# Windowed attention with sinks: the rounding and the subtraction of a finished head pair move to the front of their slots

## The chip, the cores and the metric

The kernel runs on one core of a Trainium2 chip. The metric is the device time of one launch in microseconds (us): the median of 3 runs was 3144.57 us, the runs lying between 3141.83 and 3146.22 us. One more execution was recorded by the profiler; all rows below come from it.

## What is computed

The reference is a stack of four transformer layers over 512 tokens of width 1024. The change lies in one of them only, the attention of the second layer (a window of 128 keys and one learned sink per head), which runs once:

```python
def swa_sinks(q, k, v, sinks):       # 16 query heads, 4 key/value heads, head size 64, 4 blocks of 128 queries
    s = einsum("bnqkgd,bnjkd->bnkgqj", qb, kk) * scale      # each block sees its own and the previous 128 keys
    s = where(mask, s, -inf)
    m = maximum(max(s, axis=-1), sink)
    p = exp(s - m)
    p = p / (sum(p, axis=-1) + exp(sink - m))
    out = einsum("bnkgqj,bnjkd->bnqkgd", p, vv)
mix = swa_sinks(q, k, v, od_sinks) @ od_w_out
```

## The kernel before

The program is written by hand, one instruction list per engine, with semaphores between them; nothing is reordered by a scheduler. The whole network is a list of steps (matrix products, norms, attentions), and in front of and behind each attention stands a barrier of TensorE, ScalarE and VectorE. Products that must be exact to float32 are made of two-part numbers: a "high" part, the value rounded by a ScalarE copy, and a "low" part, the value less its high part, subtracted on VectorE (here and there on GpSimd). The output of the attention needs both parts too (y_hi, y_lo), as it is the input of the next matrix product.

The function `window()`, which exists once for each engine, is the attention in question. It works in slots numbered s, one per head, and the 16 heads are staggered over them. In slot s

- TensorE transposes the probabilities of head s-2 in two halves (L1162, `turn`), each into the same PSUM bank 6, makes the scores of head s+2 in between (L1151 to L1154, `scores`), and multiplies the transposed probabilities of head s-3 with its values (L1173, `values`, 8 matmuls into bank 7). The two heads of a pair write the two halves of bank 7's partitions. Before the first head of a pair, `values` waits for the semaphore `output_low` of the pair before, since it overwrites bank 7.
- ScalarE copies each transposed half out of bank 6 (L1786, `take`), and between the two copies computes the exponentials of head s (L1775, L1777, `probs`). In every even slot it rounds the queries of a pair that comes later (L1762, `q_high`), in three slots the keys (L1767, `k_high`).
- VectorE takes the row maxima of head s+1 (L2365 to L2368, `maxima`), divides the probabilities of head s-1 by their sum (L2375 to L2382, `scale`), and in odd slots subtracts the low part of queries (L2352, `low_q`), in three slots that of keys (L2358, `low_k`).
- GpSimd copies key rows (L800) eight times in the stage; it has no part in the outputs.

A finished pair has three more steps, in every odd slot from s=5 to s=19: ScalarE rounds bank 7 into y_hi (L1791, `y_high`, waits for `values_added` of both heads), VectorE subtracts it from bank 7 into y_lo (L2386, `sub_low`, waits for `output_high`), and then `values` of the next pair may write bank 7. Both heads of pair p are multiplied with their values by the end of TensorE's slot 2p+4; the next pair's first `values` is the last thing of TensorE's slot 2p+5. Its two waits are these:

```python
pe.wait_ge(e["taken"], past(2 * h + 2))
if par == 0:
    pe.wait_ge(e["output_low"], past(pair))
```

Each engine runs its list strictly in the written order, so the place of a step in the slot decides what is held up by its wait. The scores lie in three slices of PSUM (`window_scores`, h % 3) and the probabilities in four of SBUF (h % 4), so that a head's scores, maxima, exponentials, division and transposition are spread over five slots.

Of the kernel before, what the change touches and what calls it, by code (L numbers as in the profile page):

```python
# [115 lines left out]
def program(nc, a, out):  # L116
# [9 lines left out]
    def past(n):  # L126

        return n + CR

    with ctx:  # L130
# [77 lines left out]
        def zt(k, n=1):  # L208
            return Z[:, k * S:(k + n) * S] if isinstance(k, int) else Z[:, bass.ds(k * S, n * S)]

        def zrows(rows, k):
            return Z[rows, k * S:(k + 1) * S] if isinstance(k, int) else Z[rows, bass.ds(k * S, S)]
# [6 lines left out]
        def parts(mode):  # L219

            if mode == "dil":
                last = [whi[1][:, 0:S], whi[1][:, S:2 * S], kz_last[:, 0:S], wlo[1][:, 0:S], wlo[1][:, S:2 * S], kz_last[:, S:2 * S]]
                return ([qkt(g) for g in range(3)], [qkt(3 + g) for g in range(3)],
                        [[qkt(6 + g) for g in range(3)], last[0:3]], [[qkt(9 + g) for g in range(3)], last[3:6]])
            return ([qkt(k) for k in range(2)], [qkt(2 + k) for k in range(2)],
                    [[qkt(4 + 4 * par + k) for k in range(2)] for par in range(2)],
                    [[qkt(6 + 4 * par + k) for k in range(2)] for par in range(2)])
# [433 lines left out]
        def window_scores(h, b, n=1):  # L661

            o = 2 * (h % 3) * S + 2 * P * b
            return PS[:, o + P:o + 2 * P] if b == 0 else PS[:, o:o + 2 * P * n]

        def window_probs(h, b, n=1):
            t = TMP[:, h % 4 * WIDE:(h % 4 + 1) * WIDE]
            return t[:, 0:P] if b == 0 else t[:, P + 2 * P * (b - 1):P + 2 * P * (b - 1 + n)]
# [10 lines left out]
        def window_small(h, what):  # L679

            return sums8[:, 4 + 12 * what + 4 * (h % 3):8 + 12 * what + 4 * (h % 3)]
# [732 lines left out]
        def _(act):  # L1414
# [341 lines left out]
            def window():  # L1756
                e = wn
                q_hi, _, k_hi, _ = parts("window")

                def q_high(pair):  # L1760
                    act.wait_ge(e["scores"], past(2 * pair - 2))
                    act.activation(q_hi[pair % 2], zt(pair), ACT.Copy).then_inc(e["q_high"], 1)  # L1762

                def k_high(j):
                    r = HALF[j % 2]
                    act.wait_ge(e["scores"], past(4 * j - 4))
                    act.activation(k_hi[j % 2][j % 2][r, :], zrows(r, 8 + j // 2), ACT.Copy).then_inc(e["k_high"], 1)  # L1767

                def probs(h):

                    act.wait_ge(e["neg_max"], past(h + 1))
                    act.wait_ge(e["turned"], past(2 * h - 6))
                    act.wait_ge(e["scaled"], past(h - 2))
                    small = window_small(h, 0)
                    act.activation(window_small(h, 2), small, ACT.Exp, bias=sinkb[:, h:h + 1]).then_inc(e["sink"], 1)  # L1775
                    for b in range(NB):
                        ins = act.activation(window_probs(h, b), window_scores(h, b), ACT.Exp, bias=small[:, b:b + 1],  # L1777
                                             accum_out=window_small(h, 1)[:, b:b + 1])
                    ins.then_inc(e["probs"], 1)

                def take(h, half):

                    n = len(TURNS[4 * half:4 * half + 4]) * P
                    act.wait_ge(e["turned"], past(2 * h + half + 1))
                    act.wait_ge(e["values_added"], past(h - 1))
                    act.activation(window_turned(h)[:, half * S:half * S + n], bank[6][:, 0:n], ACT.Copy).then_inc(e["taken"], 1)  # L1786

                def y_high(pair):

                    act.wait_ge(e["values_added"], past(2 * pair + 2))  # L1790
                    act.activation(ch(yhi, pair), bank[7], ACT.Copy).then_inc(e["output_high"], 1)  # L1791

                k_high(0)
                q_high(0)
                q_high(1)
                for s in range(HEADS + 4):
                    if 2 <= s < HEADS + 2:
                        take(s - 2, 0)
                    if s < HEADS:
                        probs(s)  # L1800
                    if 2 <= s < HEADS + 2:
                        take(s - 2, 1)
                    if s >= 4 and s % 2:
                        y_high((s - 4) // 2)
                    if s % 2 == 0 and s // 2 + 2 < HEADS // 2:
                        q_high(s // 2 + 2)
                    for j in range(1, 4):
                        if s == max(4 * j - 5, 0):
                            k_high(j)
# [169 lines left out]
        def _(dve):  # L1979
# [365 lines left out]
            def window():  # L2345
                e = wn
                q_hi, q_lo, k_hi, k_lo = parts("window")

                def low_q(pair):
                    dve.wait_ge(e["q_high"], past(pair + 1))  # L2350
                    dve.wait_ge(e["scores"], past(2 * pair - 2))
                    dve.tensor_tensor(q_lo[pair % 2], zt(pair), q_hi[pair % 2], ALU.subtract).then_inc(e["q_low"], 1)  # L2352

                def low_k(j):
                    r = HALF[j % 2]
                    dve.wait_ge(e["k_high"], past(j + 1))
                    dve.wait_ge(e["scores"], past(4 * j - 4))
                    dve.tensor_tensor(k_lo[j % 2][j % 2][r, :], zrows(r, 8 + j // 2), k_hi[j % 2][j % 2][r, :], ALU.subtract).then_inc(e["k_low"], 1)  # L2358

                def maxima(h):  # L2360

                    dve.wait_ge(e["scores"], past(h + 1))
                    dve.wait_ge(e["probs"], past(h - 2))
                    dve.wait_ge(e["neg_max"], past(h))
                    dve.tensor_reduce(window_max[:, 0:1], window_scores(h, 0), AX.X, ALU.max)  # L2365
                    dve.tensor_reduce(window_max[:, 1:NB], window_scores(h, 1, NB - 1).rearrange("p (b n) -> p b n", b=NB - 1), AX.X, ALU.max).then_inc(e["reduced"], 1)
                    dve.wait_ge(e["reduced"], past(h + 1))
                    dve.tensor_scalar(window_small(h, 0), window_max, sinkb[:, h:h + 1], -1.0, ALU.max, ALU.mult).then_inc(e["neg_max"], 1)  # L2368

                def scale(h):  # L2370

                    inv = window_small(h, 1)
                    dve.wait_ge(e["sink"], past(h + 1))
                    dve.wait_ge(e["probs"], past(h + 1))
                    dve.tensor_tensor(inv, inv, window_small(h, 2), ALU.add).then_inc(e["summed"], 1)  # L2375
                    dve.wait_ge(e["summed"], past(h + 1))
                    dve.reciprocal(inv, inv).then_inc(e["inverted"], 1)
                    dve.wait_ge(e["inverted"], past(h + 1))
                    dve.tensor_scalar(window_probs(h, 0), window_probs(h, 0), inv[:, 0:1], None, ALU.mult)
                    rows = window_probs(h, 1, NB - 1).rearrange("p (b n) -> p b n", b=NB - 1)  # L2380
                    by_block = inv[:, 1:NB].rearrange("p (b o) -> p b o", o=1).to_broadcast([P, NB - 1, 2 * P])
                    dve.tensor_tensor(rows, rows, by_block, ALU.mult).then_inc(e["scaled"], 1)  # L2382

                def sub_low(pair):
                    dve.wait_ge(e["output_high"], past(pair + 1))
                    dve.tensor_tensor(ch(ylo, pair), bank[7], ch(yhi, pair), ALU.subtract).then_inc(e["output_low"], 1)  # L2386

                low_k(0)
                low_q(0)
                low_q(1)  # L2390
                maxima(0)
                for s in range(HEADS + 4):
                    if s + 1 < HEADS:
                        maxima(s + 1)
                    if 1 <= s < HEADS + 1:
                        scale(s - 1)
                    if s >= 4 and s % 2:
                        sub_low((s - 4) // 2)
                    if s % 2 and s // 2 + 2 < HEADS // 2:
                        low_q(s // 2 + 2)  # L2400
                    for j in range(1, 4):
                        if s == max(4 * j - 5, 0):
                            low_k(j)
# [267 lines left out]
```

## Time and profile before

| what | value |
|---|---|
| median of 3 runs | 3144.57 us |
| the profiled execution's own time | 3139.92 us |
| its span | 3138.0 us |
| TensorE matmul busy in the span | 2925.7 us, 93% |
| VectorE, ScalarE, GpSimd busy | 1729.9, 1222.5, 1105.0 us |
| mean granted TensorE clock | 0.97 |

The span is the time from the first to the last instruction on the core; 1.9 us of the profiled execution's time lie outside of it. The attention in question runs from about 820 to 928 us. A matmul's recorded time is modelled, so a busy TensorE can hold small gaps; idle times are printed in square brackets, with the engine and line that ended them. In windows, PEclk is the granted TensorE clock as a share of 2.4 GHz: 1.00 is that, 0.50 is 1.2 GHz.

### The profile page before, as it was taken

The numbers are of one execution on the slowest core, as the hardware profiler recorded it, in microseconds if no ns is written. First come the engines' busy times: TensorE is split into PE (matmuls) and PEld (weight loads), VectorE is DVE, ScalarE is ACT, GpSimd is POOL, SyncE is SP. The second block draws the span as 40 slices with busy tenths as digits, with TensorE's granted clock in tenths as the row PEclk, the third lists the DMA queues.
The fourth block names the chain that finished last, engine by engine and source line by source line (L and its number), as shares of the span: only waits on it lengthen the run. The fifth ranks groups of instructions, "written<-read, shape, count | busy, mean of one in ns | idle before, by whom it ended". The sixth has DMA issues, their size and how long they took to land.

```text
span 3138.0 us, 39991 instructions
## 1 busy us (share of the span) xinstructions
PE 2925.7 (93%) x13704; PEld 2385.4 (76%) x13704; DVE 1729.9 (55%) x2176; ACT 1222.5 (39%) x2056; POOL 1105.0 (35%) x484
## 2 busy tenths in 40 slices
PE   5989999999879999999679999999899998999999
PEld 4767778877657888888458888888777897788887
DVE  7575757474546553764755333576275726563333
ACT  2564432233544322344443222466445654332221
POOL 3311444443214444443224444444202431044443
PEclk9998999998989999999889999999899999999999
DMA  5243445451002333332013333232102220033332
GB/s 195 83 150 124 154 128 194 141 160 63 28 21 81 94 100 94 89 94 88 1 34 94 95 98 96 88 95 89 48 1 62 88 88 8 15 100 94 94 94 94
DMA packets 364859, 278.85 MB, mean 89 GB/s; under 512 B 13363, under 2 KB 320948, under 8 KB 363700
## 3 DMA queue, kind: packets, MB, share of 16 engines
q1 hardware_dynamic: 363472, 276.76, 28.8%
q8 instruction: 79, 1.29, 0.2%
q14 instruction: 57, 0.46, 0.0%
q10 hardware_dynamic: 1251, 0.33, 0.0%
HBM read 274.96 MB, written 2.10 MB: 88 GB/s over the span
## 4 chain that ended last, share of the span: by engine, by line
PE 62%; issue 6%; DVE 3%; ACT 2%; POOL 1%; DVEq 0%; ACTq 0%; POOLq 0%
PE banks L993 12%; PE banks L988 12%; PE banks L997 12%; PE banks L945 6%; PE banks L951 6%; PE banks L948 6%; PE banks L1173 1%; PE banks L920 1%; PE banks L1355 1%; PE banks L1287 1%; PE banks L990 1%; ACT tmp L1777 0%; PE banks L1162 0%; PE banks L1335 0%; ACT tmp L1906 0%
## 5 line engine op out<-in xcount | busy, mean ns | idle before, releaser
L815 POOL TENSOR_TENSOR w_lo<-w_raw,w_hi 128x1024 fp32r<-128x1024 f32 (+1 forms) x424 | 1046.2, 2468 | 1831.2 <-ACT w_hi L1484 1830.2
L1484 ACT ACTIVATE w_hi<-w_raw 128x1024 fp32r<-128x1024 f32 (+1 forms) x424 | 445.6, 1051 | 1126.9 <-PE banks L997 824.0
L945 PE MATMUL banks<-w_hi,h_hi 128*128 128x512 f32 x960 | 387.5, 404 | 10.5 <-ACT h_hi L1661 7.2
L948 PE MATMUL banks<-w_hi,h_lo 128*128 128x512 f32 x960 | 378.7, 394 | 3.7 <-DVE h_lo L511 3.7
L951 PE MATMUL banks<-w_lo,h_hi 128*128 128x512 f32 x960 | 379.1, 395 | 0.8 <-POOL w_lo L815 0.7
L988 PE MATMUL banks<-h_hi,w_hi 128*128 128x512 f32 x1280 | 340.2, 394 | 10.0 <-ACT h_hi L1668 9.8
L993 PE MATMUL banks<-h_lo,w_hi 128*128 128x512 f32 x1280 | 319.3, 390 | 1.6 <-DVE h_lo L511 1.6
L988 PEld LDWEIGHTS banks<-h_hi,w_hi 128*128 128x128 f32 x1280 | 242.6, 190 | 65.6 <-issue 13.9
L997 PE MATMUL banks<-h_hi,w_lo 128*128 128x512 f32 x1152 | 284.5, 389 | 0.0
L993 PEld LDWEIGHTS banks<-h_lo,w_hi 128*128 128x128 f32 x1280 | 240.2, 188 | 55.2 <-DVE h_lo L511 5.7
L997 PEld LDWEIGHTS banks<-h_hi,w_lo 128*128 128x128 f32 x1152 | 216.2, 188 | 44.9
L945 PEld LDWEIGHTS banks<-w_hi,h_hi 128*128 128x128 f32 x960 | 198.0, 206 | 43.4 <-issue 12.4
L988 PE MATMUL banks<-mid_hi,w_hi 128*128 128x512 f32 x864 | 218.0, 391 | 12.8 <-ACT mid_hi L1608 6.8
L948 PEld LDWEIGHTS banks<-w_hi,h_lo 128*128 128x128 f32 x960 | 198.4, 207 | 35.9 <-DVE h_lo L511 4.2
L951 PEld LDWEIGHTS banks<-w_lo,h_hi 128*128 128x128 f32 x960 | 197.8, 206 | 36.5 <-POOL w_lo L815 2.0
L993 PE MATMUL banks<-mid_lo,w_hi 128*128 128x512 f32 x864 | 218.6, 392 | 1.3 <-DVE mid_lo L2128 1.1
L997 PE MATMUL banks<-mid_hi,w_lo 128*128 128x512 f32 x864 | 215.0, 390 | 0.0
L2145 DVE TENSOR_TENSOR xT<-banks,xT 128x512 f32 (+1 forms) x80 | 55.3, 692 | 280.6 <-PE banks L997 280.6
L988 PEld LDWEIGHTS banks<-mid_hi,w_hi 128*128 128x128 f32 x864 | 162.1, 188 | 52.3 <-ACT mid_hi L1608 9.4
L993 PEld LDWEIGHTS banks<-mid_lo,w_hi 128*128 128x128 f32 x864 | 162.7, 188 | 39.6 <-DVE mid_lo L2138 3.5
L997 PEld LDWEIGHTS banks<-mid_hi,w_lo 128*128 128x128 f32 x864 | 162.8, 188 | 33.8
L2233 DVE TENSOR_TENSOR tmp<-tmp,head_sums 128x512 f32<-128x512 f32 (+1 forms) x84 | 133.4, 1588 | 36.0 <-issue 24.5
(311 smaller groups left out, 4505.4 us busy)
## 6 DMA issues: line engine op xcount, KB each, us to landing
w_raw<-in_m_w_up SPq DMA_DIRECT2D x64, 512.0 KB, 3.9
w_raw<-in_m_w_down SPq DMA_DIRECT2D x64, 512.0 KB, 3.4
Z<-in_ada_w SPq DMA_DIRECT2D x48, 512.0 KB, 4.7
w_raw<-in_kv_w SPq DMA_DIRECT2D x48, 512.0 KB, 3.7
w_raw<-in_ffn_w_gate SPq DMA_DIRECT2D x44, 512.0 KB, 3.8
w_raw<-in_ffn_w_up SPq DMA_DIRECT2D x44, 512.0 KB, 3.8
tmp<-in_ada_w SPq DMA_DIRECT2D x32, 512.0 KB, 4.8
w_raw<-in_ffn_w_down SPq DMA_DIRECT2D x32, 512.0 KB, 3.4
```

What stands on the lines that cost most here:

```text
L815: pool.tensor_tensor(wlo[j][:, 0:n], raw[j][:, 0:n], whi[j][:, 0:n], ALU.subtract).then_inc(s_wlo, 1)
L920: mm = pe.transpose(turned(n)[:, j * P:(j + 1) * P], tmp[4 + n % 2][:, j * P:(j + 1) * P], ident)
L945: pe.matmul(t, hh, wh, start=k == 0, stop=False)
L948: pe.matmul(t, hl, wh, start=False, stop=False)
L951: mm = pe.matmul(t, hh, wl, start=False, stop=k == DC - 1)
L988: pe.matmul(g, whi[par][:, k * P:(k + 1) * P], hi[:, k * S:(k + 1) * S], start=(k == 0), stop=False)
L990: pe.matmul(g, wlo[par][:, k * P:(k + 1) * P], hi[:, k * S:(k + 1) * S], start=False, stop=False)
L993: mm = pe.matmul(g, whi[par][:, k * P:(k + 1) * P], lo[:, k * S:(k + 1) * S], start=False, stop=early and k == st.kc - 1)
L997: mm = pe.matmul(g, wlo[par][:, k * P:(k + 1) * P], hi[:, k * S:(k + 1) * S], start=False, stop=(k == st.kc - 1))
L1484: act.activation(whi[par][:, 0:kc * P], raw[par][:, 0:kc * P], ACT.Copy).then_inc(s_whi, 1)
L2145: dve.tensor_tensor(x, G[par], x, ALU.add).then_inc(evac[par], 1)
L2233: dve.tensor_tensor(by_head(tmp[4 + n % 2], w), roped, scale, ALU.mult).then_inc(h_out, 1)
```

## The change

In ScalarE's list `y_high` moves from behind the second `take` of its slot to the very front of the slot, ahead of the first `take`. In VectorE's list `sub_low` moves from behind `scale` to the place between `maxima` and `scale`. The instructions, their operands and every semaphore they wait for stay what they were; TensorE's, GpSimd's and the DMA queues' lists are the same.

```diff
@@ ScalarE, window()
                 for s in range(HEADS + 4):
+                    if s >= 4 and s % 2:
+                        y_high((s - 4) // 2)
                     if 2 <= s < HEADS + 2:
                         take(s - 2, 0)
                     if s < HEADS:
                         probs(s)
                     if 2 <= s < HEADS + 2:
                         take(s - 2, 1)
-                    if s >= 4 and s % 2:
-                        y_high((s - 4) // 2)
                     if s % 2 == 0 and s // 2 + 2 < HEADS // 2:
                         q_high(s // 2 + 2)
@@ VectorE, window()
                 for s in range(HEADS + 4):
                     if s + 1 < HEADS:
                         maxima(s + 1)
+                    if s >= 4 and s % 2:
+                        sub_low((s - 4) // 2)
                     if 1 <= s < HEADS + 1:
                         scale(s - 1)
-                    if s >= 4 and s % 2:
-                        sub_low((s - 4) // 2)
                     if s % 2 and s // 2 + 2 < HEADS // 2:
                         low_q(s // 2 + 2)
```

ScalarE's list before, from the end of slot 6 to the start of slot 8 (L1762 is q_high of slot 6, L1786 take, L1775 and L1777 probs, L1791 y_high, L1767 k_high):

```order
L1762 ACTIVATE qk_parts<-Z 128x512
L1786 ACTIVATE Z<-banks 128x512
L1775 ACTIVATE head_sums<-head_sums,sink_b 128x4
L1777 ACTIVATE tmp,head_sums<-banks,head_sums 128x128
L1777 ACTIVATE tmp,head_sums<-banks,head_sums 128x256 x3
L1786 ACTIVATE Z<-banks 128x384
L1791 ACTIVATE y_hi<-banks 128x512
L1767 ACTIVATE qk_parts<-Z 64x512
L1786 ACTIVATE Z<-banks 128x512
```

The same place of ScalarE's list in the changed kernel:

```order
L1762 ACTIVATE qk_parts<-Z 128x512
L1791 ACTIVATE y_hi<-banks 128x512
L1786 ACTIVATE Z<-banks 128x512
L1775 ACTIVATE head_sums<-head_sums,sink_b 128x4
L1777 ACTIVATE tmp,head_sums<-banks,head_sums 128x128
L1777 ACTIVATE tmp,head_sums<-banks,head_sums 128x256 x3
L1786 ACTIVATE Z<-banks 128x384
L1767 ACTIVATE qk_parts<-Z 64x512
L1786 ACTIVATE Z<-banks 128x512
```

The one instruction L1791 has moved past the six of take, probs and take; k_high (L1767) keeps its place at the end of the slot. VectorE's list at its first odd slot with an output, slot 5, as a difference (L2365, L2366 and L2368 are maxima, L2375 to L2382 scale, L2386 sub_low, L2352 low_q):

```order
 L2366 TENSOR_REDUCE head_sums<-banks 128x3
 L2368 TENSOR_SCALAR head_sums<-head_sums,sink_b 128x4
+L2386 TENSOR_TENSOR y_lo<-banks,y_hi 128x512
 L2375 TENSOR_TENSOR head_sums<-head_sums 128x4
 L2377 RECIPROCAL head_sums<-head_sums 128x4
 L2379 TENSOR_SCALAR tmp<-tmp,head_sums 128x128
 L2382 TENSOR_TENSOR tmp<-tmp,head_sums 128x768
-L2386 TENSOR_TENSOR y_lo<-banks,y_hi 128x512
 L2352 TENSOR_TENSOR qk_parts<-Z,qk_parts 128x512
 L2365 TENSOR_REDUCE head_sums<-banks 128x1
```

L2386 has moved past the four instructions of scale, which now stand behind its wait; low_q and the next slot's maxima were behind it before as well.

## Rows read from the trace of the kernel before

**Rows 1.** Waits, 850 to 928 us: who waited for whom, us, times, longest.
```profile
DVE y_lo L2386 <- ACT y_hi L1791: 33.1, 8, 10.7
PE banks L1173 <- DVE y_lo L2386: 15.4, 7, 3.0
PE banks L1162 <- ACT Z L1786: 3.1, 4, 0.8
```
**Rows 2.** Chain that ended last, 856 to 865 us: start, us, what.
```profile
858.39 0.60 PE banks L1162 x4
...
859.79 1.72 ACT tmp L1777 x8
861.51 0.38 ACT Z L1786
861.89 0.50 ACT y_hi L1791
862.39 0.02 issue
862.41 0.70 DVE y_lo L2386
```
**Rows 3.** Timeline of slot 7: start, us, engine, line, operation, forms [idle before].
```profile
856.66 1.73 PE L1173 MATMUL banks<-Z 128*64 128x256 f32 x8
857.63 0.23 DVE L2368 TENSOR_SCALAR head_sums<-head_sums,sink_b 128x4 f32<-128x4 f32 x1
857.77 0.16 DVE L2375 TENSOR_TENSOR head_sums<-head_sums 128x4 f32<-128x4 f32 x1
858.32 0.66 PE L1162 MATMUL banks<-squares,tmp 128*128 128x128 f32 x4
858.38 0.95 DVE L2382 TENSOR_TENSOR tmp<-tmp,head_sums 128x768 f32<-128x768 f32 x1
859.01 0.60 ACT L1786 ACTIVATE Z<-banks 128x512 f32<-128x512 f32 x1 [1.02 <-PE banks L1162]
860.66 0.49 PE L1162 MATMUL banks<-squares,tmp 128*128 128x128 f32 x3
861.76 0.62 ACT L1791 ACTIVATE y_hi<-banks 128x512 fp32r<-128x512 f32 x1
862.41 0.69 DVE L2386 TENSOR_TENSOR y_lo<-banks,y_hi 128x512 fp32r<-128x512 f32 x1 [3.08 <-ACT y_hi L1791]
863.25 2.39 PE L1173 MATMUL banks<-Z 128*64 128x256 f32 x8 [2.10 <-DVE y_lo L2386]
```
**Rows 4.** Timeline of slots 14 to 19, columns as in rows 3.
```profile
902.88 1.73 PE L1173 MATMUL banks<-Z 128*64 128x256 f32 x8
...
906.12 0.52 PE L1162 MATMUL banks<-squares,tmp 128*128 128x128 f32 x3 [0.78 <-ACT Z L1786]
...
909.62 3.22 PE L1173 MATMUL banks<-Z 128*64 128x256 f32 x8 [2.98 <-DVE y_lo L2386]
...
915.47 3.25 PE L1173 MATMUL banks<-Z 128*64 128x256 f32 x8
...
920.10 0.52 PE L1162 MATMUL banks<-squares,tmp 128*128 128x128 f32 x3 [0.78 <-ACT Z L1786]
...
922.50 4.09 PE L1173 MATMUL banks<-Z 128*64 128x256 f32 x16 [1.89 <-DVE y_lo L2386]
```
**Rows 5.** Windows between y_high starts: length, PE, PEld, DVE, ACT, POOL busy, PEclk, DMA.
```profile
850.77:861.76 10.99, 8.89 (x62) 6.96 (x62) 6.76 (x16) 6.77 (x26) 0.00 (x0) 1.00 0.01 2
861.76:874.34 12.58, 10.48 (x62) 8.14 (x62) 9.59 (x17) 7.61 (x27) 4.00 (x3) 0.86 0.14 42
885.33:897.88 12.55, 10.46 (x62) 8.21 (x62) 6.76 (x16) 6.35 (x25) 0.00 (x0) 0.86 0.00 1
908.13:921.04 12.91, 9.44 (x30) 5.30 (x30) 2.09 (x5) 2.70 (x6) 0.00 (x0) 0.60 0.00 1
839.00:850.20 11.20, 11.17 (x83) 8.91 (x81) 8.04 (x20) 8.95 (x33) 1.69 (x2) 1.00 0.01 2
```

## The prediction, made before the changed kernel ran

> **What bounds the kernel now.** I read the list of waits of the attention stage first, then the chain that ended last through one odd slot, then the timeline of that slot and of the end of the stage, and last the windows with the granted clock. Over the whole span TensorE is 93% busy, so only time in which TensorE itself stands still, or runs at a lower clock, can be won.
>
> In the waits the reader is to see a relay [rows 1]: VectorE's y_lo (L2386) waits 33.1 us for ScalarE's y_hi (L1791), and TensorE's values (L1173) wait 15.4 us in 7 times for y_lo. VectorE's 33.1 us cost nothing by themselves; TensorE's 15.4 us do. The chain shows that they lie on the path that sets the end [rows 2]: from a transposition (858.39) it goes over ScalarE's exponentials (1.72), its second take (0.38) and y_hi (0.50) to y_lo (0.70), and then to values. The timeline tells what the chain does not [rows 3]: y_hi starts at 861.76, but its data, the values of head 3, were complete at 856.66 + 1.73 = 858.39. For 3.37 us it waits for nothing but its place in ScalarE's list. TensorE ends its last transposition of the slot at 860.66 + 0.49 = 861.15 and starts the next values at 863.25, which is the 2.10 us in brackets. There are 7 such waits: five of 2.10, then 2.98 and 1.89 [rows 3, 4]; 5 x 2.10 + 2.98 + 1.89 = 15.37, the 15.4 of rows 1. The last output (slot 19) has no values behind it and gains nothing.
>
> **The change, part by part.** No instruction is added or taken away, and no semaphore changes.
>
> *y_hi to the front of its slot.* It can now start when the values of slot s-1 end, 858.39 in slot 7, and takes 0.62. The row of y_lo starts 862.41 - 861.76 = 0.65 after the start of y_hi, so y_lo would start near 859.05 and end near 859.05 + 0.69 = 859.74. TensorE asks for it at 861.15, so 1.4 us are spare and the whole wait of 2.10 goes. Queued behind y_hi's wait is the first take. It waits for the transposition at 858.32 + 0.66 = 858.98 anyway and started at 859.01 after 1.02 us of idleness [rows 3]; y_hi ends at 858.39 + 0.62 = 859.01. So y_hi fits into the idle time of ScalarE nearly exactly; up to 0.05 us for the start of y_hi may be lost per slot. The bounds: 0 and, if nothing overlapped, 0.62 x 7 = 4.3 us. I take 0.05 x 7 = 0.4, since the row has the idle time right there; up to slot 13 the scores ahead of the second transposition may hide even that, which I do not count on.
>
> *y_lo ahead of scale.* VectorE had finished maxima at 857.63 + 0.23 = 857.86 and ran scale from 857.77 to 858.38 + 0.95 = 859.33, that is 1.56 us [rows 3]. Now it stands at y_lo's wait until 859.05, so scale runs from 859.74 to 861.30, 2.0 us later than before. Who waits for it is the first transposition of the next slot. With the wait gone, TensorE does the values from 861.15 to 862.88 and asks then: 1.6 us are spare. Behind scale stand low_q and the next maxima, whose users are one slot and more away. VectorE has 6.76 us of work in a pair of slots of 10.99 [rows 5] and the pair shrinks to 10.99 - 2.10 = 8.89, so it does not become the bound; nor does ScalarE with 6.77. The second window holds 9.59 us of VectorE work, part of it the key halves of slot 7, and is the tightest place, but it occurs once and its maxima are needed a slot later. Cost: 0; the upper bound is 2.0 - 1.6 = 0.4 us in each of 7 slots if the spare time did not exist at all for reasons the trace hides, 2.8 us.
>
> *The end of the stage.* From slot 14 TensorE has no scores left and its slot is short: from values at 902.88 to the end of the second transposition at 906.12 + 0.52 = 906.64 are 3.76 us, with 0.78 of waiting for take in it [rows 4]. With y_hi at the front, y_lo(5) ends about 1.4 us into slot 15 and scale(14) some 3.0 us into it (0.65 + 0.69 + 1.56), still under 3.76. So both late waits, 2.98 and 1.89, go as well.
>
> *The clock.* Two windows from one y_hi to the next contain the same work at two clocks [rows 5]: 10.99 us at 1.00, and 12.58 and 12.55 at 0.86. The lower one of the two levels, 1.2 GHz, cost 1.59 and 1.56 us. The third case is the end: values to the end of the second transposition takes 3.76 us at full clock; from 909.62 to 915.47 are 5.85 and from 915.47 to 920.62 are 5.15 us, and the last 16 matmuls took 4.09 against 2 x 1.73 = 3.46 [rows 4]. That is 2.09 + 1.39 + 0.63 = 4.1 us. Together 1.59 + 1.56 + 4.1 = 7.3 us. What did TensorE do before each fall? It had just stood still: for 2.10 us before the values at 863.25, which took 2.39 instead of 1.73 [rows 3], and for 2.98 us before those at 909.62, which took 3.22 [rows 4]. Where it had no such gap, as from 839 to 850 with 11.17 of 11.20 us busy, the clock stayed at 1.00 [rows 5]; and in slots 14 and 15, with short gaps alone, the values at 902.88 still took 1.73 and the transposition at 906.12 its 0.52, the same as at full clock [rows 3, 4]. As the change takes away just the long gaps, I expect most of the falls to go. Bounds: 0 (all falls stay) and 7.3 us; I take 6.8, as a fall may still come at the very end of the stage, where TensorE waits for the last y_hi and y_lo.
>
> A page speaks against this last step. The Trainium skill, "TensorE: Matmul & The Clock Gate", section "A second HAM failure mode: psum-queue depth-cycling", says that short pauses between groups of matmuls, if frequent enough, make the clock fall and rise again and again. By it the end of the stage, with its gap in every slot, would stay at the low level, and 4.1 of the 7.3 us would not come. The trace disagrees as far as the gap of 0.78 in front of 906.12 goes: the transposition behind it still took 0.52.
>
> **Sum.** 15.4 (waits) + 6.8 (clock) - 0.4 (ScalarE's front) = 21.8 us. Against the profiled execution's own 3139.92 this is 3118.1. The median of the runs shown is 4.65 us above that execution, so 3144.57 - 21.8 = 3122.8 us.
>
> **Rivals.**
> *A: only the waits go, the clock falls as often as before.* For it: the falls could follow a rhythm that does not care for these gaps, since only two of the three falls that I can price follow a wait of 2.10 us, and of the five such waits three brought none (the first window of rows 5 holds one at 1.00). Against it: 839 to 850. Gain 15.4 - 0.4 = 15.0, time 3129.6.
> *B: the front place costs.* y_hi delays the take, the take the exponentials and, in the short slots, the second transposition; scale comes late by its 0.4. At the bounds, 4.3 + 2.8 = 7.1 us of the 15.4 come back and the clock gives nothing: 3144.57 - 8.3 = 3136.3. For it: both moved steps now stand ahead of work that was ready without them. Against it: 1.02 us of idle time on ScalarE and 1.6 us spare for scale.
> The Trainium skill has a sentence on this, in "TensorE: Matmul & The Clock Gate", section "Architectural detail: the array is 16× 32×32, not 1× 128×128": ScalarE and VectorE take their instructions strictly first in, first out. So a wait at the front does hold everything behind it, as this trace agrees with (y_lo's 3.08 us of idleness with low_q behind it, rows 3).
> *C: slower.* One mechanism: scale(s-1), now behind y_lo, becomes what the first transposition of slot s+1 waits for, and since values, y_hi, y_lo and scale then form a ring, each pair of slots is as long as that ring. It takes effect once scale ends more than 1.6 us later than I reckon and makes the kernel slower once it is more than 1.6 + 2.1 = 3.7 us later. At 1 us beyond that point it would cost 7 x 1.0 = 7 us: 3151.6. Against it: the ring's pieces are 0.65 + 0.69 + 1.56 = 2.90 us and a slot is 4.49 (861.15 + 1.73 - 858.39).
> *D: nothing changes*, because the gain is taken up at the barrier behind the stage. The matrix product there starts when y_lo of the last pair is written, so nothing else is late: 3144.6.
>
> **How the numbers follow.** Forecast 62%, with its own range 3118 to 3127; A 23%; B 9%; D 3%; C 3%. The 80% range takes the forecast and A and leaves B, C and D out: 3117 to 3132. By less than 0.2%, 6.3 us, a measurement of this kernel cannot tell a change from none. Faster by more than that are the forecast, A and most of B (93%), within it D and a rest of B (4%), slower C (3%).
>
> **What would show it.** Right: no wait of L1173 for y_lo, or only tenths of a us; y_hi starts within 0.1 us of the end of the second values of its pair; the distance between starts of y_hi is about 8.9 us up to slot 13 and 7.4 after; the first take waits about 0 instead of 1.02 us; from 850 us to the end of the stage the granted clock is 1.00 or nearly; the stage ends some 22 us earlier, and everything behind it keeps its length. Wrong on the clock, if the stage shortens by 15 us and windows at 0.5 remain (rival A). Wrong on VectorE, if L1162 shows a new wait for L2382 in even slots (B or C). The prediction as a whole fails if L1173 still waits more than 1 us in most odd slots.

## The result: 3116.25 us, 0.9 per cent faster, and the profile after

| | before | changed kernel |
|---|---|---|
| median, runs beside each other | 3144.03 us (4 runs) | 3116.25 us (4 runs, 3115.93 to 3119.99) |
| ratio, 95% interval | | 0.9913 (0.9897 to 0.9929) |
| span of the profiled execution | 3138.0 us | 3114.1 us |

The gain is 27.8 us by the medians and 24 us by the two profiled executions; 21.8 was forecast, and the time lies 0.75 us below the range. The interval of the ratio is 22 to 32 us of gain. The waits and the clock of the stage came as forecast. What was off is the step from one profiled execution to the median: before's median lay 4.65 us above its profiled execution, the changed kernel's 0.32 us (3116.25 - 3115.93). The experiments look for the reason.

The waits of the stage after, 847 to 906 us, columns as in rows 1:

```profile
DVE y_lo L2386 <- ACT y_hi L1791: 14.1, 7, 3.8
ACT y_hi L1791 <- PE banks L1173: 5.8, 7, 2.1
PE banks L1162 <- ACT Z L1786: 3.1, 4, 0.8
PE banks L1162 <- DVE tmp L2382: 0.9, 1, 0.9
```

TensorE's 15.4 us for y_lo [rows 1] are gone, row and all. In their place y_hi itself waits, 5.8 us in 7 times, for the values: it now asks as soon as the data can be there. One new wait has come, 0.9 us of the transpositions for scale. Slot 7 after, in the timeline, against rows 3:

```profile
854.58 1.73 PE L1173 MATMUL banks<-Z 128*64 128x256 f32 x8
856.24 0.66 PE L1162 MATMUL banks<-squares,tmp 128*128 128x128 f32 x4
856.35 0.60 ACT L1791 ACTIVATE y_hi<-banks 128x512 fp32r<-128x512 f32 x1 [0.43 <-PE banks L1173]
856.93 0.60 ACT L1786 ACTIVATE Z<-banks 128x512 f32<-128x512 f32 x1
856.98 0.69 DVE L2386 TENSOR_TENSOR y_lo<-banks,y_hi 128x512 fp32r<-128x512 f32 x1 [1.19 <-ACT y_hi L1791]
857.59 0.15 DVE L2375 TENSOR_TENSOR head_sums<-head_sums 128x4 f32<-128x4 f32 x1
...
858.58 0.49 PE L1162 MATMUL banks<-squares,tmp 128*128 128x128 f32 x3
859.00 1.73 PE L1173 MATMUL banks<-Z 128*64 128x256 f32 x8
```

y_hi starts 0.04 us after the values end (854.58 + 1.73 = 856.31). The first take starts 0.03 us after its transposition (856.24 + 0.66 = 856.90), as before: y_hi fits the idle time. y_lo ends at 857.67, and the next values follow the last transposition without a gap. The stage in windows, from the y_hi of one pair to the next and as a whole:

```profile
847.51:856.35 8.84, 8.84 (x63) 6.96 (x64) 6.77 (x16) 6.87 (x25) 0.00 (x0) 1.00 0.01 3
856.35:865.19 8.84, 8.80 (x62) 6.85 (x62) 7.25 (x14) 7.60 (x26) 4.05 (x3) 1.00 0.00 0
847.51:905.10 57.59, 51.90 (x348) 38.96 (x348) 39.26 (x88) 40.94 (x138) 4.05 (x3) 1.00 0.04 10
```

Where rows 5 have 10.99 to 12.58 us for a pair, these have 8.84, nearly all of it TensorE's (8.84 and 8.80); and the granted clock is 1.00 over the whole stage, where rows 5 have 0.86 in two windows and 0.60 in a third. The front section names for GpSimd in this stage only its copies of key rows; it also starts there on the weights of the next product (L815), which will matter below.

### The profile page after: what moved, and what is told of

It is laid out like the page before. It is cut to its first block, busy times and chain, and to the rows that moved or that the text cites. A ratio compares the mean times of both kernels' runs of the same rounds, so it can differ in the third digit from the quotient of the medians.

```text
span 3114.1 us, 39991 instructions
## 1 busy us (share of the span) xinstructions
PE 2916.9 (94%) x13704; PEld 2380.7 (76%) x13704; DVE 1728.8 (56%) x2176; ACT 1223.0 (39%) x2056; POOL 1104.5 (35%) x484
## 4 chain that ended last, share of the span: by engine, by line
PE 62%; issue 6%; DVE 3%; ACT 2%; POOL 1%; DVEq 0%; ACTq 0%; POOLq 0%
PE banks L993 12%; PE banks L988 12%; PE banks L997 12%; PE banks L945 6%; PE banks L951 6%; PE banks L948 6%; PE banks L920 1%; PE banks L1355 1%; PE banks L1173 1%; PE banks L1287 1%; PE banks L990 1%; PE banks L1162 0%; PE banks L1335 0%; ACT tmp L1906 0%; PE banks L1338 0%
## 5 line engine op out<-in xcount | busy, mean ns | idle before, releaser
L815 POOL TENSOR_TENSOR w_lo<-w_raw,w_hi 128x1024 fp32r<-128x1024 f32 (+1 forms) x424 | 1045.9, 2467 | 1808.9 <-ACT w_hi L1484 1807.9
L2233 DVE TENSOR_TENSOR tmp<-tmp,head_sums 128x512 f32<-128x512 f32 (+1 forms) x84 | 133.3, 1587 | 36.0 <-issue 24.4
```

Of the source, the lines that this page charges most:

```text
L815: pool.tensor_tensor(wlo[j][:, 0:n], raw[j][:, 0:n], whi[j][:, 0:n], ALU.subtract).then_inc(s_wlo, 1)
L2233: dve.tensor_tensor(by_head(tmp[4 + n % 2], w), roped, scale, ALU.mult).then_inc(h_out, 1)
```

## The experiments

Three distances between the starts of two fixed matmuls, from the traces, serve as a yardstick: A from matmul 3300 to 3712 (in before 837.11 to 926.21 us, the stage from the scores of slot 2 to the last values), B from 3712 to 3950 (to 992.16, the end of the stage, the product and the norm behind it), C from 6150 to 6600 (1498.10 to 1630.87, the attention of the third layer). "Own" is the profiled execution's time.

```
                     A     B     C      own
before              89.1  65.9  132.8  3139.92
before, again       87.0  68.6  136.0  3144.11
before, third       89.1  65.9  132.8  3138.50
before, fourth      90.5  68.6  136.0  3142.94
before, fifth       87.2  68.6  136.0  3141.95
only VectorE's half 90.5  68.6  136.3  3146.27
y_hi behind probs   80.1  66.0  132.2  3128.04
y_hi behind take    70.1  65.9  135.8  3123.04
only ScalarE's half 66.7  65.9  135.0  3120.31
changed             66.0  65.9  132.2  3115.93
changed, again      66.0  66.0  135.9  3119.21
changed, timed      66.0  65.9  132.2  3116.02
two banks           64.7  66.9  136.1  3120.01
split late          63.8  66.0  135.0  3113.36
```

**Only ScalarE's half.**
```diff
 ScalarE:  for s in range(HEADS + 4):
+              if s >= 4 and s % 2: y_high((s - 4) // 2)      # ahead of take; sub_low stays behind scale
```


> Only ScalarE's half of the change: y_high at the front of its slot, sub_low still behind scale. Theory (the place of y_hi in ScalarE's list is the whole relay): VectorE ends scale 0.94 us after the values of the pair (859.33 against 858.39), y_lo would then start at about 1.0 us instead of 0.65 us and still end 1.1 us before TensorE asks; no wait of L1173 for y_lo up to slot 13, at most 0.1 us in slots 15 and 17; time as the changed kernel, 3116 to 3119 us. Rival (VectorE's half is needed too): waits of L1173 for y_lo of 0.5 us and more remain in most odd slots, time 3122 us or more.

Measured: 3117.15 us, ratio 0.9911 (0.9894 to 0.9927). The theory holds for the time: ScalarE's place is the relay, and it alone brings the whole gain, as far as these intervals tell. One wait for y_lo stayed, in slot 9, where the theory had none:

```profile
863.27 2.13 DVE L2379 TENSOR_SCALAR tmp<-tmp,head_sums 128x128 f32<-128x128 f32 x1
...
869.82 1.70 PE L1173 MATMUL banks<-Z 128*64 128x256 f32 x8 [0.65 <-DVE y_lo L2386]
```

It is in the slot after a division row that took 2.13 us instead of 0.29. VectorE's half is worth this 0.65 us, and no more (A 66.7 against 66.0); both kernels have the wait of 0.85 or 0.86 us for scale besides.

**Only VectorE's half.**
```diff
 VectorE:      maxima(s + 1)
+              if s >= 4 and s % 2: sub_low((s - 4) // 2)     # y_high stays at the end of ScalarE's slot
               scale(s - 1)
```


> Only VectorE's half: sub_low between maxima and scale, y_high still at the end of its slot. Theory: y_hi starts as late as before, so y_lo too, and the 7 waits of L1173 stay at 2.1, 3.0 and 1.9 us, 15 us in sum; scale now ends 0.65 + 0.69 + 1.56 = 2.9 us after the start of y_hi, which is 864.7 against TensorE's question at 864.98, so it just fits: time 3144 us, within 3 us. Rival (the late scale becomes a new wait): L1162 waits for L2382 in even slots, up to 1 us each, time up to 3151 us.

Measured: 3142.02 us, ratio 0.9995 (0.9985 to 1.0006): no change. Its waits:

```profile
PE banks L1173 <- DVE y_lo L2386: 15.3, 7, 3.0
PE banks L1162 <- DVE tmp L2382: 0.8, 1, 0.8
```

All seven waits are there, and the late scale shows once, as a wait of 0.8 us. So a subtraction that waits for a late rounding is no better off in front.

**The kernel before and the changed kernel, again.** No edit in either.

> The kernel before once more, for a second profile of it. Theory (the falls of the clock follow the waits of TensorE, but which of the seven waits brings one differs from execution to execution): TensorE waits 15.4 us for y_lo again, and windows at 0.5 stand in the stage at another count or other places than 864, 888, 908 and 922; total at the low clock in the stage between 13 and 35 us. Rival (the falls belong to fixed places of the program): the same four stretches at the same places, 20 us in sum.

> The changed kernel once more. Theory: from 842 us to the end of the stage no window at 0.5 at all, the stage ends at 905 us as in the first profile, within 0.3 us. Rival (a fall can come without a wait): at least one stretch at 0.5 between 842 and 905 us and a stage longer by 1.5 us.

Measured: before 3144.11 us; in the stage the low clock stood near 865, 899, 909 and 919 instead of 864, 888, 909 and 922, in sum 20.5 us again. So which of the waits a fall comes behind differs from execution to execution. The last of these stretches, from 919.2 to 929.4 us, runs 5.1 us past the last values, into B. The changed kernel: 3119.21 us, no window at 0.5 between 842 and 905, A 66.0 as in its first profile. Its 3.3 us over the first execution lie not in the stage but mostly in C, 135.9 against 132.2.

**y_hi behind the first take.**
```diff
               take(s - 2, 0)
+              if s >= 4 and s % 2: y_high((s - 4) // 2)
               probs(s)
```


> y_high between the first take and probs, sub_low behind scale as before. Theory (only y_hi ready before TensorE's last transposition of the slot counts): y_hi starts 1.2 us after the values of its pair, y_lo ends 0.2 us before TensorE asks in slots up to 13; waits of L1173 for y_lo are 0 to 0.2 us there and 0.6 to 0.7 us in slots 15 and 17, 1.5 to 2.5 us in sum; no fall of the clock in the middle of the stage; time 3117 to 3121 us. Rival (the very front is needed): waits of 1 us and more in each odd slot, time over 3125 us.

Measured: 3120.98 us, ratio 0.992 (0.9904 to 0.9935), within the theory; waits for y_lo 2.0 us in 3 times. But one fall came, behind a wait of 0.69 us at the end of the stage, in slot 15:

```profile
895.14 3.15 PE L1173 MATMUL banks<-Z 128*64 128x256 f32 x8 [0.69 <-DVE y_lo L2386]
```

3.15 instead of 1.73 us. A is 4.1 us longer than in the changed kernel: 2.0 are waits for y_lo, 0.5 a longer wait for scale (1.33 instead of 0.86), and the rest, 1.6 us, is what the fall costs by this difference.

**y_hi behind probs.**
```diff
               probs(s)
+              if s >= 4 and s % 2: y_high((s - 4) // 2)
               take(s - 2, 1)
```


> y_high between probs and the second take, sub_low behind scale as before: y_hi starts only 0.38 us earlier than before. Theory (falls of the clock follow TensorE's waits): waits of L1173 for y_lo are 1.7 us up to slot 13 and 2.6 and 1.5 us after, 12.7 us in sum; windows at 0.5 in the stage remain, 13 to 31 us in sum; time 3141 to 3143 us. Rival (the falls need the full 2.1 us of standing still): waits as said but hardly a fall, time 3134 us or less.

Measured: 3127.31 us, ratio 0.9943 (0.9928 to 0.9958). The theory missed the time and the falls. The rival's time (3134 us or less) and its "hardly a fall" came true; its reason, that a fall needs a wait of the full 2.1 us, did not, as the 0.69 us of the kernel before this one show:

```profile
849.80 1.70 PE L1173 MATMUL banks<-Z 128*64 128x256 f32 x8 [1.71 <-DVE y_lo L2386]
...
902.30 2.12 PE L1173 MATMUL banks<-Z 128*64 128x256 f32 x8 [2.59 <-DVE y_lo L2386]
```

The waits are as said, 11.9 us in 7 times, but with 1.7 instead of 2.1 us each the middle of the stage ran at 1.00; only 6.8 us of low clock are left, behind the 2.59. A is 80.1 us, 8.5 less than the mean of before, for 3.5 us less waiting: some 5 us are the clock. With B and C (1.5 and 2.5 us under their means of before) this is 12.5 us, against 13.4 between this profiled execution and the mean of the five of before (3128.04 and 3141.5), and against 18.0 between the medians. Most of the rest lies in executions of before that are longer than its profiled ones: the nine runs beside this one took 3143.3 to 3147.9 us.

**The changed kernel, timed longer.** No edit.

> The changed kernel in more rounds, since its first median lies 27.8 us under that of before while the two profiled executions differ by 24.0. Theory (the first 24 us are the stage; the rest is the spread of both kernels' executions, 3137.7 to 3147.5 for before): the difference settles at 23 to 26 us, ratio 0.9917 to 0.9927. Rival (something outside the profiled difference is won in unprofiled executions): the difference stays at 27 us or more.

Measured: 3116.09 us (3114.74 to 3123.01) against 3145.34, ratio 0.9914 (0.9901 to 0.9928). The theory that the medians would come together at 23 to 26 us did not come true: the difference is 29.3 us, after 27.8, though the interval (23 to 31 us) holds both.

**Two banks for the last transpositions.**
```diff
-  pe.wait_ge(e["taken"], past(2 * h + half))
+  pe.wait_ge(e["taken"], past(2 * h if h >= 13 else 2 * h + half))
-  bank[6]
+  bank[2] if h >= 13 and half else bank[6]          # TensorE's write and ScalarE's take
```


> The changed kernel, with the second halves of the transpositions of heads 13, 14 and 15 written to PSUM bank 2, which the scores no longer use then, instead of bank 6; the second transposition no longer waits for the first take. Theory: the 0.78 us that TensorE waits in slots 15, 16 and 17 go, and ScalarE becomes the limit of slots 15 and 16 at 3.5 and 2.9 us; gain 1 to 2.3 us over the changed kernel, 3114 to 3116 us. Rival (ScalarE's list is the limit there already): gain under 0.5 us.

Measured: 3119.15 us, ratio 0.9910 (0.9895 to 0.9925). A is 64.7, so 1.3 us are won in the stage, within the theory's 1 to 2.3 us; the time was forecast at 3114 to 3116 us and missed that, and does not tell this kernel from the changed one. The profiled execution has C in the long form (136.1), and a B of 66.9 us that comes up again below.

**And the split of the next weights held back.**
```diff
 GpSimd, end of window():
+  pool.wait_ge(e["scaled"], past(16))               # on top of the two banks
```


> The changed kernel with two edits: the second transpositions of heads 13 to 15 in bank 2, and GpSimd's subtraction L815 for the next matrix product held back until the last scale. Theory: the scale row of slot 8 that took 2.14 us beside L815 takes 0.29 again, so L1162 no longer waits 0.9 us for it; with the gaps of the three late slots gone the part from the first values wait to the end of the stage is 2.1 us shorter than in the changed kernel (53.0 to about 50.9 us between the same two matmuls); time 3112 to 3116 us, if the attention of the third layer falls into its two forms (132 or 136 us) as often as in the changed kernel. Rival (another operand, not GpSimd, held that row): L2379 still takes 2 us and L1162 waits.

The changed kernel had these rows beside each other in slot 8:

```profile
862.64 2.36 POOL L815 TENSOR_TENSOR w_lo<-w_raw,w_hi 128x1024 fp32r<-128x1024 f32 x1 [0.24 <-POOL qk_parts L800]
862.74 0.18 DVE L2377 RECIPROCAL head_sums<-head_sums 128x4 f32<-128x4 f32 x1
862.95 2.14 DVE L2379 TENSOR_SCALAR tmp<-tmp,head_sums 128x128 f32<-128x128 f32 x1
...
866.01 0.66 PE L1162 MATMUL banks<-squares,tmp 128*128 128x128 f32 x4 [0.86 <-DVE tmp L2382]
```

VectorE's division starts 0.3 us into GpSimd's subtraction and ends 0.1 us after it, and TensorE waits 0.86 us for what follows. With the subtraction held back the same division (five lines further down in that kernel) takes

```profile
863.92 0.29 DVE L2384 TENSOR_SCALAR tmp<-tmp,head_sums 128x128 f32<-128x128 f32 x1
```

The theory holds; as the two banks alone left the wait of 0.86 us for scale in place, it is the held-back subtraction that removes it. Measured: 3114.93 us (3111.93 to 3118.78), ratio 0.9916 (0.9902 to 0.9929), A 63.8: 2.2 us less than the changed kernel in the stage, 0.9 of them over the two banks alone. Its median is the lowest, but the runs of before beside it were faster too (3143.55 us), and by the ratio it can't be told from the changed kernel (0.9913 and 0.9914).

**Three more profiles of the kernel before.** No edit.

> A third profile of the kernel before. Theory (the first one was a lucky execution): stage 87 to 90 us between the same two matmuls, and of the two later parts that come in two forms at least one is in the long form: the product and norm behind the stage 68.6 instead of 65.9 us, the attention of the third layer 136 instead of 132.5; own time 3142 us or more. Rival (what the first profile shows is typical): 65.9 and 132.5 again, own time 3140 us.

> A fourth profile of the kernel before; the same theory and rival as for the third.

> A fifth profile of the kernel before; the same theory and rival as for the third.

Measured: 3138.50, 3142.94 and 3141.95 us. The fourth and fifth have both later parts in the long form, as the second had, though the fifth's own time lies just under the 3142 us of the theory; the third is like the first, as the rival had it. So the first was one of the two luckier of five. What the two forms of B are, the window from 925 to 995 us shows, for the first, the second and the fourth profile of before:

```profile
925.00:995.00 70.00, 62.43 (x259) 49.12 (x256) 38.86 (x38) 25.05 (x31) 27.51 (x10) 0.95 0.24 72
```
```profile
925.00:995.00 70.00, 62.40 (x246) 48.80 (x247) 38.85 (x38) 24.30 (x31) 27.47 (x10) 0.89 0.23 69
```
```profile
925.00:995.00 70.00, 62.82 (x247) 49.13 (x248) 38.86 (x38) 24.31 (x31) 27.47 (x10) 0.90 0.24 70
```

TensorE is busy for the same time and gets through 12 or 13 matmuls less, at a granted clock of 0.89 or 0.90 instead of 0.95. The long form is a longer time at the low clock, and it lies in two places. The first is the stretch right behind the last values, with the first matmuls of the next product. Here are its first eight matmuls for the first and second profile of before and for the changed kernel:

```profile
928.10 2.08 PE L988 MATMUL banks<-y_hi,w_hi 128*128 128x512 f32 x8 [1.51 <-DVEq L1992]
```
```profile
926.48 3.46 PE L988 MATMUL banks<-y_hi,w_hi 128*128 128x512 f32 x8 [1.50 <-DVEq L1992]
```
```profile
905.07 2.08 PE L988 MATMUL banks<-y_hi,w_hi 128*128 128x512 f32 x8 [1.51 <-DVEq L1992]
```

The whole stretch in windows, for the first and second profile of before:

```profile
926.21:931.83 5.62, 4.11 (x19) 3.25 (x18) 1.18 (x2) 1.66 (x2) 2.39 (x1) 1.00 0.00 0
```
```profile
924.34:931.63 7.29, 5.79 (x19) 4.43 (x18) 1.18 (x2) 1.65 (x2) 2.37 (x1) 0.65 0.04 13
```

The same work takes 1.7 us longer at a clock of 0.65. That is the end of the stage's own last stretch at the low clock, which in the three long profiles of before (and in that of VectorE's half alone) is 10.2 us long and runs over into B; the edit takes it away. The second place is around the norm, 1.0 us, and this the edit does not touch. The rest of B for the first and second profile of before and for the two banks:

```profile
931.83:992.16 60.33, 54.27 (x221) 42.80 (x220) 36.15 (x35) 22.35 (x28) 24.88 (x9) 0.94 0.25 74
```
```profile
931.63:992.92 61.29, 55.16 (x222) 42.88 (x221) 36.15 (x35) 22.34 (x28) 24.87 (x9) 0.92 0.24 71
```
```profile
907.53:968.79 61.26, 55.16 (x222) 42.91 (x221) 36.10 (x35) 22.35 (x28) 24.84 (x9) 0.92 0.25 73
```

The forms of C go with the granted clock as well, though not strictly (only ScalarE's half has 135.0 us at 0.89). For the first and second profile of before and for the first two of the changed kernel:

```profile
1498.10:1630.87 132.77, 96.75 (x451) 66.04 (x452) 88.70 (x168) 69.66 (x196) 18.71 (x22) 0.89 0.03 9
```
```profile
1498.89:1634.88 135.99, 99.75 (x451) 67.98 (x452) 88.66 (x168) 69.67 (x196) 18.66 (x22) 0.87 0.03 8
```
```profile
1475.02:1607.24 132.22, 96.94 (x451) 66.21 (x452) 88.56 (x168) 69.78 (x196) 18.25 (x22) 0.91 0.03 9
```
```profile
1474.00:1609.90 135.90, 99.61 (x451) 67.76 (x452) 88.64 (x168) 69.57 (x196) 18.66 (x22) 0.87 0.03 8
```

## Why the prediction was right and wrong, point by point

*The relay and the place of y_hi: right.* Seven waits, 15.4 us, all gone; y_hi starts when it was reckoned to (0.04 us after the values), costs the take nothing, and ScalarE's half alone does it. The 0.4 us set aside for ScalarE's front were not spent.

*y_lo ahead of scale: "cost 0", upper bound 2.8 us. Nearly right.* It cost 0.9 us once. The tightest place was named, the pair with the key halves, but its reason was missed: GpSimd's subtraction holds a VectorE row for its length. Before the change the same subtraction sat on the last row of a maxima, as the timeline of the kernel before shows:

```profile
865.63 2.36 POOL L815 TENSOR_TENSOR w_lo<-w_raw,w_hi 128x1024 fp32r<-128x1024 f32 x1 [0.24 <-POOL qk_parts L800]
865.94 2.07 DVE L2368 TENSOR_SCALAR head_sums<-head_sums,sink_b 128x4 f32<-128x4 f32 x1
```

Nobody waited for those maxima in this profile; in the changed order a scale stands there, for which TensorE does wait. Rival B's mechanism took effect once and at a third of the 2.8 us.

*The clock: right, and sized nearly right.* 7.3 us were read from the rows and 6.8 taken. In the changed kernel no fall is left in the stage in three profiles. Compared with the profile on which the prediction rests, A fell by 89.1 - 66.0 = 23.1 us: 15.4 of waits less the new 0.9, 7.3 of clock, and 1.3 that were mis-sized. The largest piece of these is the last values, in the changed kernel

```profile
900.91 2.65 PE L1173 MATMUL banks<-Z 128*64 128x256 f32 x16
```

where I had set 2 x 1.73 = 3.46: the second head's matmuls begin while the first head's still run. The forecast for the stage was 21.8. Rival A, the waits alone, is refuted by the windows, C and D by the time. The rule of the Trainium skill that short frequent pauses make the clock fall and rise ("TensorE: Matmul & The Clock Gate", "A second HAM failure mode: psum-queue depth-cycling") did not come true at the end of the stage, where pauses of 0.78 us remain in each slot from 14 to 17 at 1.00; with 0.69 us on top of them, in the kernel with y_hi behind take, one fall of 3.4 us came. What decides between the two, no run here shows.

*The step that failed is the last one of the sum*, in its words "The median of the runs shown is 4.65 us above that execution, so 3144.57 - 21.8", together with "everything behind it keeps its length". I took the distance between the profiled execution and the median for a constant that both kernels share. It is not one: 4.65 us in before, 0.32 in the changed kernel, which is 4.3 of the 6.5 us by which the median missed 3122.8. The other 2.2 us lie between the two profiled executions (3115.93 instead of 3118.1), 1.3 of them in the stage and 0.6 in C. In before, B and C are in their long forms in three of five profiles; in the changed kernel B never is and C in one of three. By the means of the table A fell by 88.6 - 66.0 = 22.6, B by 67.5 - 65.9 = 1.6 and C by 134.7 - 133.4 = 1.3 us: 25.5 together. Of B's 1.6 us some 1.0 (1.7 us in three of five) is the low clock that the stage handed on and that the edit removes, so the stage is worth more than A shows; the other 0.6 and C's 1.3 us are places that the edit does not touch. The means of the own times, 3141.5 and 3117.1, differ by 24.4. In addition each median is the middle of several forms: the changed kernel's ten runs lie six at 3114.7 to 3116.4 and four at 3119.2 to 3123.0, so its median falls into the lower group, while 26 of the 35 runs of before lie above 3143. These times, too, go with the clock: its mean over the run is 0.970 in the run of before that took 3137.7 us, 0.968 in those of 3143.3 to 3145.2, and 0.966 or 0.967 in those above 3147. (Four runs at 0.960 to 0.962, of 3138.6 to 3146.1 us, stand apart; two profiled executions at such a mean have 44 us at the low clock near the start, see the last section.) The low end of the range, 3117.0, left no room for this, and that is why the time fell out of it.

*What stays open.* Why the long forms around the norm and in C come in some executions and not in others. A stage that ends at the low clock is not needed for the one at the norm: the kernel with two banks has no fall in its stage and shows it all the same (0.92 in its window). Whether it makes it more likely, three profiles of the changed kernel can't tell. The rest between 24.4 us in the profiled executions and 27 to 29 in the medians was not located either, and lies within the interval. Nothing new is needed for it: by an estimate from the profiles of before, the longest that they show of each part (837.4 us up to matmul 3300, A 90.5, B 68.6, C 136.0, 505.9 between B and C, 1507.4 behind C, 1.9 outside of the span) add up to 3147.7 us, the length of its longer runs.

## What to carry to other kernels

Where an engine waits for a short step on another engine, look first at when that step's data were ready and when it was its turn; if the data were there 3 us earlier, only its place in the list is wrong, and the right one is where its engine was idle anyway. A pause of TensorE on the path is worth more than its length if the clock falls behind it, here half as much again (7.3 us of clock on 15.4 of waits); read both from the same rows, and follow the low clock past the end of the part that you change. And do not carry a difference from one profiled execution over to a median: profile the kernel before two or three times, and let the range be as wide as its own executions.

## What the runs showed of the hardware that was not expected

- A VectorE row of 0.29 us (L2379, one operand in SBUF and one column of scalars) took 2.14 us when it began inside a GpSimd subtraction of 2.36 us, and ended 0.1 us after it; with the subtraction elsewhere it took 0.29 again. In before the row held is L2368, of only 128x4, which took 2.07 us instead of 0.23, so size does not decide it: both are TENSOR_SCALAR. The RECIPROCAL ahead of L2379 (L2377, 128x4), which began beside the same subtraction, kept its 0.18. The Trainium skill has the shared interface ("GPSIMD Engine Reference", "8. Key points": GpSimd shares its SBUF interfaces with VectorE, with contention for instructions in a two-port mode or with two SBUF inputs); the trace agrees that there is contention, 2.14 us against 0.29; to which of the two kinds these rows belong, no run here shows.
- The falls of the clock are not proportional to the waiting. With waits of 2.1 us in every second slot (2.98 and 1.89 at the end) there were 20 to 31 us at 1.2 GHz, with 1.7 us 6.8, all behind the longest of its waits (2.59), with a total of 2.0 us 3.4, with a single one of 0.65 us or none 0.
- Two of the five profiles of before ran at the low clock for 44 us near their start and were none the slower for it, 3138.50 and 3141.95 us. For the first of them the window from 0 to 50 us shows a granted clock of 0.66 and 16 us of TensorE work in those 50:

```profile
0.00:50.00 50.00, 16.10 (x68) 13.29 (x68) 38.10 (x50) 9.45 (x16) 15.78 (x13) 0.66 0.70 264
```
